# Reordering ScalarE, VectorE and TensorE steps in two attention stages of a three-block transformer kernel

## The reference, cut to what matters

```python
# first block, nsa(): 8 heads of 64, in 2 groups; three branches share the queries
p_c = softmax over 31 compressed keys;      o_c = p_c @ Vc       # branch 0
p_s = softmax over the (all 8) 64-key blocks; o_s = p_s @ Vsel   # branch 1
p_w = softmax over the last 512 keys;       o_w = p_w @ Vwin     # branch 2
out = gate0 * o_c + gate1 * o_s + gate2 * o_w
...
# second block, neighbourhood_attention(): 8 heads; 512 tokens are an 8 x 64 grid
s_win  = q . k over an 8 x 16 window of the grid + a bias of its own for each offset
s_meta = q . k over 16 meta tokens
p = softmax([s_win, s_meta]);  out = p_win @ v_win + p_meta @ v_meta
```

## Time and profile before

| | |
|---|---|
| median of 3 runs | 1692.14 us (1690.14 to 1698.04) |
| the profiled execution, its own time | 1694.75 us |
| its span in the trace | 1693.4 us (1.35 us lie around it) |
| TensorE busy | 1613.7 us, 95% |
| VectorE, ScalarE, GpSimd busy | 874.4 us (52%), 634.1 us (37%), 50.4 us (3%) |
| chain that ended last | TensorE 89%, ScalarE 4%, VectorE 3%, issue 2% |
| mean granted TensorE clock | 0.981 |
| first block's attention | about 224 to 367 us of the span |
| neighbourhood heads, layer a and layer b | about 952 to 1029 us and 1444 to 1524 us |

### The profile page before, as it was taken

One profiled execution on the slowest core, in us unless ns is written; L12 is line 12 of the kernel. 1 busy time (PEld: TensorE's weight loads), 2 busy tenths in 40 slices (PEclk: granted clock), 3 DMA queues, 4 the chain that ended last, 5 costly groups with the idle time before them and its releaser, 6 DMA issues.

```text
span 1693.4 us, 24835 instructions
## 1 busy us (share of the span) xinstructions
PE 1613.7 (95%) x10381; PEld 1363.0 (80%) x10381; DVE 874.4 (52%) x1558; ACT 634.1 (37%) x1124; POOL 50.4 (3%) x51
## 2 busy tenths in 40 slices
PE   7999978899999999999999989999999998999997
PEld 5898755577888888889888878999987887678886
DVE  4434655556654655855545455435545445445543
ACT  5232245444322333743334343223333333443233
POOL 0000001000000000011000000000010000000000
PEclk9999989999999999999999899999999999999999
DMA  6234400015323332241212202223422103212331
GB/s 193 76 79 85 114 14 1 26 48 138 100 90 85 98 100 99 75 88 59 67 51 43 59 14 75 76 88 113 100 50 71 55 26 56 57 39 92 95 112 50
DMA packets 175600, 125.22 MB, mean 74 GB/s; under 512 B 48752, under 2 KB 172272, under 8 KB 175488
## 3 DMA queue, kind: packets, MB, share of 16 engines
q1 hardware_dynamic: 175488, 123.63, 26.3%
HBM read 121.52 MB, written 2.10 MB: 73 GB/s over the span
## 4 chain that ended last, share of the span: by engine, by line
PE 89%; ACT 4%; DVE 3%; issue 2%; POOL 0%; DVEq 0%; ACTq 0%; POOLq 0%
PE bank L586 70%; PE bank L2729 2%; PE bank L2761 2%; PE bank L2741 2%; ACT probs L1536 1%; PE bank L3137 1%; PE bank L3100 1%; PE bank L2637 1%; PE bank L1606 1%; PE bank L3116 1%; PE bank L1252 1%; PE bank L2588 1%; PE bank L1656 1%; ACT w_hi L533 1%; PE bank L2272 1%
## 5 line engine op out<-in xcount | busy, mean ns | idle before, releaser
L586 PE MATMUL bank<-h_hi,w_hi 128*128 128x512 f32 (+2 forms) x920 | 329.6, 378 | 7.8 <-issue 4.4
L542 DVE TENSOR_TENSOR w_lo<-w_raw,w_hi 128x2048 fp32r<-128x2048 f32 (+2 forms) x117 | 241.1, 2061 | 183.4 <-ACT w_hi L533 183.0
L586 PE MATMUL bank<-h_lo,w_hi 128*128 128x512 f32 (+2 forms) x920 | 324.6, 373 | 0.0
L586 PE MATMUL bank<-h_hi,w_lo 128*128 128x512 f32 (+2 forms) x920 | 323.5, 372 | 0.0
L533 ACT ACTIVATE w_hi<-w_raw 128x2048 fp32r<-128x2048 f32 (+2 forms) x117 | 201.1, 1719 | 74.5 <-DMA w_raw<-w_in 35.9
L586 PEld LDWEIGHTS bank<-h_hi,w_hi 128*128 128x128 f32 (+1 forms) x920 | 168.4, 191 | 50.8 <-issue 17.3
L586 PEld LDWEIGHTS bank<-h_hi,w_lo 128*128 128x128 f32 (+1 forms) x920 | 167.9, 191 | 30.9
L586 PEld LDWEIGHTS bank<-h_lo,w_hi 128*128 128x128 f32 (+1 forms) x920 | 167.8, 191 | 30.4 <-issue 0.5
L586 PE MATMUL bank<-g_hi,w_hi 128*128 128x264 f32 (+1 forms) x752 | 184.2, 311 | 1.4 <-DVE z_a L2211 0.9
L586 PE MATMUL bank<-g_lo,w_hi 128*128 128x264 f32 (+1 forms) x752 | 181.7, 307 | 0.0
L586 PE MATMUL bank<-g_hi,w_lo 128*128 128x264 f32 (+1 forms) x752 | 181.0, 307 | 0.0
(11 more groups left out here) (574 smaller groups left out, 2625.3 us busy)
## 6 DMA issues: line engine op xcount, KB each, us to landing
w_raw<-w_in SPq DMA_DIRECT2D x45, 1024.0 KB, 5.3
w_raw<-w_up SPq DMA_DIRECT2D x32, 512.0 KB, 4.9
w_raw<-w_in SPq DMA_DIRECT2D x40, 256.0 KB, 4.6
w_raw<-w_down SPq DMA_DIRECT2D x8, 1024.0 KB, 5.2
w_raw<-w_out SPq DMA_DIRECT2D x8, 1024.0 KB, 5.2
w_raw<-w_out SPq DMA_DIRECT2D x8, 512.0 KB, 3.5
w_raw<-w_ple_gate SPq DMA_DIRECT2D x4, 1024.0 KB, 5.1
w_raw<-w_o_attn SPq DMA_DIRECT2D x8, 512.0 KB, 3.5
```

The source lines that it names most:

```text
L542: DV.e.tensor_tensor(wlo[u % RING][:, 0:n], raw[u % RING][:, 0:n], whi[u % RING][:, 0:n].bitcast(F32), ALU.subtract).then_inc(*w_low(u))
L586: ins = PE.e.matmul(out, stationary[a](k), moving[b](k)[i], start=first and n == 0, stop=last and n == 2)
```

## The change

In NSA, TensorE's order stays as it is. On ScalarE and VectorE `filled` is replaced by a new helper, `nsa_steps`, that takes its stages in any order and gives the fill behind them. Within step s the orders are:

| | before | after |
|---|---|---|
| ScalarE | exp of branch 0 (s), factors (s-3), exps (s), fill, wide (s-1), copy (s-2), value part (s-3) | factors (s-3), copy (s-2), exps (s), wide (s-1), fill, value part (s-3) |
| VectorE | score (s), fill, inverse (s-1), copy (s-2), out (s-3) | score (s), inverse (s-1), copy (s-2), fill, out (s-3) |

The first unit's widening is done at step 2 right behind its copy. In NA all three engines get `apart=True`: score (s), fill due at item s-1, turn (s-2), value (s-3), instead of score (s), fill due at item s, turn (s-1), value (s-2).

```diff
@@ ac_nsa_score
-            factors = i > 2 and is_last(units_n[i - 3])
             if br == 0:
                 AC.wait_ge(*n_soft.at("less", t))
                 AC.e.activation(sc[0][:, 0:256], sc[0][:, 0:256], ACT.Exp).then_inc(*n_exp(t, 0, 0))
-            if factors:
-                ac_nsa_factors(units_n[i - 3])
-            if br == 0:
                 return
@@ ac_nsa_turn
-            for ready in exped_with(i):
-                ac_nsa_wide(ready)
-            if i + 2 >= len(units_n) and is_last(units_n[i - 1]):
+            if i and is_last(units_n[i - 1]):
                 ac_nsa_factors(units_n[i - 1])
             if i > 1:
                 AC.wait_ge(*n_valued.at(i - 2))
             AC.wait_ge(*n_turned.at(i, 0))
             AC.e.activation(dst, src, ACT.Copy).then_inc(*n_flip_a(i, 0))
+            if i == 0:
+                ac_nsa_wide(unit)
+
+        def ac_nsa_widen(unit):
+            i = number_n[unit]
+            for ready in exped_with(i):
+                if ready != units_n[0]:
+                    ac_nsa_wide(ready)
@@ new
+        def nsa_steps(fill, value, *stages_):
+            given = 0
+            for step in range(len(units_n) + 3):
+                for stage_, behind in stages_:
+                    if 0 <= step - behind < len(units_n):
+                        stage_(units_n[step - behind])
+                while given < 11 * min(step, len(units_n)) // len(units_n):
+                    next(fill)
+                    given += 1
+                if step > 2:
+                    value(units_n[step - 3])
@@ ac_nsa
-            filled(units_n, first_steps(fill, 11), 11, ac_nsa_score, ac_nsa_turn, ac_nsa_value, apart=True)
+            nsa_steps(fill, ac_nsa_value, (ac_nsa_turn, 2), (ac_nsa_score, 0), (ac_nsa_widen, 2))
@@ dv_nsa
-            filled(units_n, first_steps(fill, 11), 11, dv_nsa_score, dv_nsa_turn, dv_nsa_value, apart=True)
+            nsa_steps(fill, dv_nsa_value, (dv_nsa_score, 0), (dv_nsa_turn, 2))
@@ pe_na, ac_na, dv_na alike
-            filled(items_a, all_of(fill, first_steps(mix, mixed_in_na(l))), 2 + mixed_in_na(l), score, turn, value)
+            filled(items_a, all_of(fill, first_steps(mix, mixed_in_na(l))), 2 + mixed_in_na(l), score, turn, value, apart=True)
```

## The result

| | before | after |
|---|---|---|
| median | 1691.14 us (4 runs, 1689.31 to 1698.04) | 1671.88 us (4 runs, 1670.41 to 1674.83) |
| ratio after / before | | 0.9884, 95% interval 0.986 to 0.9908 |
| span of the profiled execution | 1693.4 us | 1673.5 us |
| TensorE busy | 1613.7 us (95%) | 1606.2 us (96%) |

The changed kernel was timed once more later: 1677.75 us in the median of 6 runs (1672.32 to 1680.99), ratio 0.9926 (0.9905 to 0.9946) to a before of 1690.67. The ten runs together have a median of 1675.2. So the gain is 13 to 19 us, and the two medians of one kernel differ by 6 us. The mean granted clock differs too: 0.987 in the mean of the first four runs, 0.984 in that of the six.

The account below looks back on a forecast made before the run. TensorE was taken to bound the kernel (89% of the chain that ended last), so only its waits and lowered clock could give. NSA 10.5 (9.0 waits, 1.5 clock) plus NA 3 made 13.5: 1692.1 to 1678.5 us, range 1668 to 1689.

Parts of the forecast that it names:

- Copy ahead of exponentials: NSA, ScalarE: the copy no longer waits behind the exponentials, which move back with 3.2 us to spare before TensorE needs them.
- Slower by that path: Rival: late exponentials on ScalarE come onto TensorE's path in NSA, 23 steps each paying a copy; 1705 us, chance 0.05.
- The sum of waits, 9.0 us: NSA: TensorE's waits for ScalarE's copies shrink by 2.9 + 1.8 + 1.6 + 1.4 + 1.3 = 9.0 us.
- The first place: NSA's first copy wait, 4.66 us at 235.82: the copy now comes between 16 exponentials; 1.4 us goes.
- the odd steps: NSA, three steps with an odd dense k: copy wait turns into one for `n_out`, about 1.5 us each; together 1.3 goes.
- The factor waits: Sign of a wrong prediction: TensorE's waits for ScalarE's factors in NSA growing well over 2.8 us.
- The clock in NSA, 1.5 us: The second slow stretch of TensorE's clock in NSA goes, worth 1.5 us; the first and third stay.
- GpSimd against VectorE: NSA: one stretched VectorE operation and half of another go; add L1683 exposed up to 1.3 us at four places, not summed.
- NA, waits: NA: waits for exponentials in mid-stage go (4.7 and 1.6 us); new waits for `tile_done` add 4.0, following scores 0.6.
- NA, sum: NA gains 3.2 us, rounded to 3: layer a 2.3, layer b 0.1, and 0.4 each at the stage start.
- The sign named last: Sign of a wrong prediction: new slow stretches in NA, where a 1.0 us wait stands in each of the first two tiles.
- The rival in which the clock stays up too: Less idle time keeps TensorE's clock up in NSA and at NA's starts: gain 18 to 28, about 1669 us; chance 0.17.

Follow-up runs that it names:

- out_first: The changed kernel with VectorE's branch output put ahead of its fill in NSA; 1663.94 us in 5 runs, ratio to before 0.9833.
- nsa_only: The changed kernel with NA put back as before, so only the NSA reordering; 1680.73 us against 1690.25, ratio 0.994.
- after_again: The changed kernel once more, unchanged, for a second trace and more runs; 1677.75 us in 6 runs, ratio 0.9926.
- after_shift: The changed kernel with 12 extra matmuls, result thrown away, ahead of the first product of the residual stage between the layers; 1677.83 us, ratio 0.9941.
- meta_late: The changed kernel with a tile's meta scores in NA made behind that tile's first pair of scores, one step later; 1671.82 us, ratio to before 0.9875.
- na_only: The changed kernel with NSA put back as before, so only the NA reordering; 1681.77 us, ratio 0.9949.
- shift: The kernel before with 12 extra matmuls, result thrown away, ahead of the first product of the residual stage between the layers; 1688.93 us against 1691.80, ratio 0.9983.
- fill_idle: The changed kernel with six extra matmuls, result thrown away, where TensorE waits near the start of NSA; 1673.63 us, ratio 0.9907.

## Why the prediction was right

The forecast was 1678.5, 13.5 us off the median, with 1674 to 1684 as the forecast's own range and 1668 to 1689 as the whole. The first median, 1671.9, lies in the whole range and 2 us outside the forecast's own; the second, 1677.8, and that of all ten runs, 1675.2, lie in both. The mechanism in NSA was right. That the sum came out was in part luck: NA gave half of its share by the edit, and the clock made up the rest. Taken by its steps:

- **Copy ahead of exponentials.** Right. No wait for `probsT` on ScalarE is left, and the exponentials moved back do not hold TensorE up: L1532 is no releaser of it in NSA. Slower by that path did not come.
- **The sum of waits, 9.0 us.** 23.8 us of waits became 15.2: 8.6. The first place was to give 1.4: from the first score product to that of unit 4 it was 17.13 us (240.56 - 223.43) and is 15.82, 1.3. In the odd steps the copy's wait turned into one for `n_out`, as written; about 1.5 us each was forecast, 2.3, 0.8 and 2.0 were found. `out_first`, in which it is gone, shows that this wait came from the fill's place in the list.
- **The factor waits.** They were named as a sign of a wrong prediction if they grew well over 2.8 us, and they grew to 6.0 in L1602. That sign was badly chosen: the steps above had already put the factor copy behind 16 exponentials and behind the `m feat` fills, and the sum had the price in it. The list of signs was not made from the sum.
- **The clock in NSA, 1.5 us.** The second slow stretch went, as forecast (243 to 259 us: 1.00), the first (3.4 us shorter in the first trace) and the third stayed. New ones behind 313 and 341 us, ahead of which TensorE now waits 0.8 and 2.0 us, were not in the sum. In the first trace they took the gain back (27.3 us slow in all, where it was 23.9); in `nsa_only`, `after_again` and `after_shift` only the one behind 313 us is there, and shorter (3.4 us). NSA gave 8.2 us in two traces (after, `meta_late`) and 11.1 in these three; 10.5 was forecast. In `nsa_only` the 11.1 comes with the same slow time as before and with 10.0 us less waiting. So it was not the 1.5 us for the clock that filled the sum: the order itself gave more than the 9.0.
- **GpSimd against VectorE.** The operation that took 1.44 us beside GpSimd's low part takes 0.42 in every case now, and L1685, the add that I held to be exposed, 0.69 in every case. One short operation of 0.17 us (L1572, which was L1576; two inputs) was stretched to 1.24 beside GpSimd's low part at 248.29 us; before, the same operation had been stretched twice, to 0.72 and, at 268.96 us, where the prediction has its second stretch, to 1.03. What the Trainium skill says in "SBUF — State Buffer", "Who interferes with whom", agrees with these. On the add it is not tested: no GpSimd operation ran beside any of its eight cases, so the price of up to 1.3 us was not paid because the two never met.
- **NA, waits.** The waits for exponentials went. The wait for `tile_done` came four times, 0.85 us each, 3.4 in all; 4.0 was forecast, from the copy of 0.69 in the earlier trace rows. The following scores waited 0.16 or 0.17 in three places (0.2 forecast). One of 0.74 us in layer a was missed: VectorE's biased scores of item 9 stand behind a weight split. The rows of VectorE show it:

```profile
975.37 2.29 DVE L542 TENSOR_TENSOR w_lo<-w_raw,w_hi 128x2048 fp32r<-128x2048 f32 x1 [2.42 <-ACT w_hi L533]
977.58 0.70 DVE L2225 TENSOR_TENSOR z_a<-bank,norm_row_a 128x528 f32<-128x528 f32 x1
978.20 0.42 DVE L3265 CUSTOM_DVE_ANT_0 na_probs_a<-bank,na_bias_a 128x256 f32<-128x256 f32 x1
```

- **NA, sum.** 3.2 us was forecast, 1.5 + 1.7 = 3.2 measured, but not with the same parts: layer a 1.5 for 2.7, layer b 1.7 for 0.5, the latter with one fall of the clock less at its start, which is worth about as much. So the edit's own part in NA is some 1.6 us, half of the forecast, and the agreement of the sums is luck. The sign named last, new slow stretches in NA, did not come.
- **What was in no term.** The 3.1 us between the layers. The prediction took all that is outside the two stages as unchanged. With them the sum would have been 16.6 us, between the gains of the two medians.

The rival in which the clock stays up too had its gain at 18 to 28. By the first median alone (19.3 us) it would be the case that came; in the traces it is not, since in NSA, where it saw most of that gain, the clock stood at 1.2 GHz at least as long as before in the first trace. The clock did stay up more in the pieces around NSA and NA.

## What to carry to other kernels

When a fill is moved behind a copy in an engine's list, look at what stands behind the fill: here it was the operation that frees an accumulator bank, and putting that ahead too was worth another 8 to 11 us, some 5 of them the waits and the rest the clock. A list of waits gives the size of an edit only for its own stage; cut the traces at the same instructions and compare the pieces that the edit does not touch before a gain is credited to it. Where two engines' lists hand a split from one to the other, look at both: with ScalarE's order alone, 8.5 us of waits for VectorE's copies came in the place of ScalarE's. And put the mean granted clock of every run beside its time before two medians are compared: here it accounted for nearly all of the gain of `na_only` and for most of the difference between the two medians of one kernel.

## What the runs showed of the hardware

A fall of TensorE's clock in a piece whose instructions do not change can be turned off or on by 1.5 us of work ahead of the place (`shift`, `after_shift`), and costs 1.5 to 1.7 us each time: between NSA and NA the traces have 586.5, 588.1 and 589.7 us with 0, 3.4 and 6.8 us at 1.2 GHz. The times of these two pieces agree within 0.4 us from trace to trace once the slow time is the same. A wait that goes can give more than its length where the clock had fallen behind it, but need not: `out_first` took NSA down by 10.2 us for 6.6 us less waiting against the first trace of the changed kernel, and by 7.3 for 7.0 against the second. And the same wait of 2.3 us stands in front of a fall in the trace of the changed kernel and in front of none in that of `fill_idle`.
